# Rotary embedding's swapped halves: products on TensorE, or SBUF-to-SBUF copies with signed sine tables

## The reference, cut to what matters

```
x1, x2 = jnp.split(xa, 2, axis=-1)
return jnp.concatenate([x1 * cos - x2 * sin, x1 * sin + x2 * cos], axis=-1)
```

## Time and profile before

| | |
|---|---|
| median of 3 executions | 3674.78 us (3674.26 to 3675.93) |
| the profiled execution | 3672.84 us |
| its span | 3671.0 us |
| TensorE busy | 3589.8 us, 98% |
| VectorE, ScalarE, GpSimd busy | 51%, 41%, 10% |
| granted TensorE clock, mean | 0.993 |
| DMA | 337 MB, 92 GB/s in the mean |

### The profile page before, as it was taken

The page is one execution under the profiler, slowest core; times in us unless marked ns, Lnnn a source line. Parts: engine busy times, 40 slices in busy tenths (PEclk is TensorE's granted clock), DMA queues, the critical chain, the costliest instruction groups (busy, mean ns, idle before and its releaser), DMA issues.

```text
span 3671.0 us, 45622 instructions
## 1 busy us (share of the span) xinstructions
PE 3589.8 (98%) x18488; PEld 3002.9 (82%) x18488; DVE 1888.5 (51%) x3061; ACT 1506.3 (41%) x2534; POOL 382.5 (10%) x305
## 2 busy tenths in 40 slices
PE   8999999999999999999999999999999999999999
PEld 6898889999979777888757678888886777888887
DVE  4738797666665465445554443433346444343333
ACT  4245544444452463233455342332335634234232
POOL 0000042222210000000100101110100000111011
PEclk8999999999999999999999999999999999999999
DMA  6510232222244232233211223333321122332222
GB/s 254 177 47 1 107 129 64 69 69 70 62 165 138 70 118 88 90 103 101 69 49 53 84 86 96 100 104 92 98 89 52 47 85 72 100 104 94 98 93 86
DMA packets 112530, 337.12 MB, mean 92 GB/s; under 512 B 11840, under 2 KB 29120, under 8 KB 111808
## 3 DMA queue, kind: packets, MB, share of 16 engines
q1 hardware_dynamic: 103824, 301.70, 25.8%
q10 hardware_dynamic: 8496, 32.51, 2.5%
HBM read 330.49 MB, written 2.10 MB: 91 GB/s over the span
## 4 chain that ended last, share of the span: by engine, by line
PE 84%; DVE 6%; ACT 2%; issue 1%; ACTq 0%; DVEq 0%
PE ps L803 53%; PE ps L1167 8%; PE ps L1219 5%; PE ps L856 4%; PE ps L839 2%; PE ps L1532 1%; PE ps L1331 1%; PE ps L1322 1%; PE ps L1343 1%; PE ps L1073 1%; PE ps L1535 1%; PE ps L1576 1%; PE ps L1590 1%; PE ps L1005 1%; PE ps L1549 1%
## 5 line engine op out<-in xcount | busy, mean ns | idle before, releaser
L2694 DVE TENSOR_TENSOR wlo<-raw,whi 128x1024 fp32r<-128x1024 f32 (+3 forms) x583 | 620.7, 1067 | 638.1 <-ACT whi L1701 632.9
L1701 ACT ACTIVATE whi<-raw 128x1024 fp32r<-128x1024 f32 (+3 forms) x583 | 524.4, 902 | 723.5 <-PE ps L803 433.9
L803 PE MATMUL ps<-bh,whi 128*128 128x512 f32 x1248 | 496.4, 398 | 0.1
L803 PE MATMUL ps<-bh,wlo 128*128 128x512 f32 x1248 | 486.7, 390 | 0.5 <-DVE wlo L2694 0.5
L803 PE MATMUL ps<-bl,whi 128*128 128x512 f32 x1248 | 486.3, 390 | 0.0
L803 PEld LDWEIGHTS ps<-bh,whi 128*128 128x128 f32 x1248 | 234.7, 188 | 58.7 <-issue 8.1
L803 PEld LDWEIGHTS ps<-bl,whi 128*128 128x128 f32 x1248 | 234.8, 188 | 51.0 <-issue 3.4
L803 PEld LDWEIGHTS ps<-bh,wlo 128*128 128x128 f32 x1248 | 234.5, 188 | 50.3 <-DVE wlo L2694 1.0
L803 PE MATMUL ps<-ah,whi 128*128 128x384 f32 (+1 forms) x768 | 252.4, 369 | 8.0 <-DVE mod L2754 5.2
L803 PE MATMUL ps<-ah,wlo 128*128 128x384 f32 (+1 forms) x768 | 248.2, 363 | 0.1
L803 PE MATMUL ps<-al,whi 128*128 128x384 f32 (+1 forms) x768 | 248.0, 363 | 0.0
(11 more groups left out here) (480 smaller groups left out, 7391.1 us busy)
## 6 DMA issues: line engine op xcount, KB each, us to landing
raw<-weights_d SPq DMA_DIRECT2D x431, 512.0 KB, 3.5
aw<-ada_d ACTq DMA_DIRECT2D x56, 512.0 KB, 3.7
aw<-ada_d SPq DMA_DIRECT2D x40, 512.0 KB, 8.2
raw<-weights_d SPq DMA_DIRECT2D x80, 256.0 KB, 2.6
raw<-weights_d SPq DMA_DIRECT2D x44, 192.0 KB, 2.3
x<-nab_d SPq DMA_DIRECT2D x24, 256.0 KB, 2.8
x<-x_t_d SPq DMA_DIRECT2D x4, 1024.0 KB, 5.8
dt<-rtab_d SPq DMA_DIRECT2D x16, 256.0 KB, 2.9
```

The source lines that it names most:

```text
L803: m = e.matmul(p[:, 0:n], tiles(w, i)[:, k, :], xs[:, x0 + k, c0:c0 + n], start=pi == 0 and k == 0 and ti == 0, stop=i == job and k == kt ...
L1701: e.activation(flat(WHI, key), src, ACT.Copy).then_inc(q.did("hi", key))
L2694: e.tensor_tensor(flat(WLO, key), src, flat(WHI, key).bitcast(F32), ALU.subtract).then_inc(q.did("lo", key))
```

## The change

The products with PG and PR are taken out. In their place ScalarE, having evacuated a tile, issues four DMAs that copy 32 partitions of 512 fp32 values (64 KB) each to the place of the other half, in linear attention from the tile into gtr, in retention from RAW2 into RTM. The minus sign moves into the sine tables: in the constant SIN, and in the frequencies from which the kernel computes SINR. VectorE multiplies gtr or RTM by the sine in place; GpSimd's multiply by the cosine, which overwrites the source of the copies, waits for their landing. For tile 0 of retention ScalarE issues the copies after the end of stick-breaking attention. VectorE's and GpSimd's instructions are as many as before and in the same order.

```
-        cos[d], sin[d] = np.cos(ang), np.sin(ang)
+        cos[d], sin[d] = np.cos(ang), np.sin(ang) * (-1 if d % 64 < 32 else 1)
-    iv[:, 1] = np.tile(ir, 4)
+    iv[:, 1] = np.tile(ir, 4) * np.where(np.arange(128) % 64 < 32, -1, 1)
+    turned_in = [nc.alloc_semaphore(f"turned_in{i}") for i in range(4)]
+    swapped_in = [nc.alloc_semaphore(f"swapped_in{i}") for i in range(2)]
 # pe_program, linear attention
-        def rope(ct):
-            p = bank(4 + ct % 2, ("rtmp", ct))
-            q.wait_ge(("qk", ct), ("cg",))
-            e.matmul(p, PG, (Qt if ct < 4 else Kt)[:, ct % 4, TC:], start=True, stop=True, skip_group_check=True
-                     ).then_inc(q.did("ropemm", ct))
         lin_pair(["gla_w_in", "gla_w_in"], H, hr, HALF)
-        rope(0)
         for ct in range(2, 8):
             lin("gla_w_in", H, hr, HALF)
-            rope(ct - 1)
         lin("gla_a_w1", H, hr, HALF)
-        rope(7)
 # pe_program, retention
-            rotate(6, ("rq", l, 0), PR, RAW2[0], ("rraw", l, 0, 0))
-            rotate(7, ("rk", l, 0), PR, RAW2[1], ("rraw", l, 0, 1))
...
                 lin("w_in_2", B, br, ONE)
-                rotate(0, ("rq", l, j + 1), PR, RAW2[0], ("rraw", l, j + 1, 0))
                 ret_values(j, 2)
-                rotate(1, ("rk", l, j + 1), PR, RAW2[1], ("rraw", l, j + 1, 1))
                 lin("w_in_2", B, br, ONE)
 # act_program
+        def swap_halves(dst, src, sem, *name):
+
+            for to in range(0, 128, 32):
+                fro = to ^ 32
+                e.dma_start(dst[to:to + 32, :], src[fro:fro + 32, :]).then_inc(q.lands(sem, *name), 16)
+
         def evac_qk(i, ct):
...
             q.note("qk", ct)
+            q.wait_ge(("qk", ct), *([("rope", ct - 4)] if ct >= 4 else []))
+            swap_halves(GTR[ct % 4], (Qt if ct < 4 else Kt)[:, ct % 4, TC:], turned_in[ct % 4], "turned", ct)
...
+            def ret_swap(j, n):
+
+                q.wait_ge(("rraw", l, j, n), *([] if j else f))
+                swap_halves(RTM[n], RAW2[n], swapped_in[n], "swapped", l, j, n)
+
             def ret_raw(j, n):
...
                 q.note("rraw", l, j, n)
+                if j:
+                    ret_swap(j, n)
...
             q.note(f"end_sb{l}", "act")
             f = fence(f"end_sb{l}")
+            for n in range(2):
+                ret_swap(0, n)
 # dve_program
         def rope(ct):
             x = (Qt if ct < 4 else Kt)[:, ct % 4, TC:]
-            q.wait_ge(("ropemm", ct), ("cg",), *(f0 if ct < 4 else [("rope", ct - 4)]))
-            e.tensor_tensor(GTR[ct % 4], PS[4 + ct % 2], SIN, ALU.mult).then_inc(q.did("rtmp", ct))
+            q.wait_ge(("turned", ct), ("cg",))
+            e.tensor_tensor(GTR[ct % 4], GTR[ct % 4], SIN, ALU.mult).then_inc(q.did("rtmp", ct))
             q.wait_ge(("rcos", ct), ("rtmp", ct))
...
-                name, dst, b = (("rq", RQ), ("rk", RK))[n] + (n if j else 6 + n,)
+                name, dst = (("rq", RQ), ("rk", RK))[n]
                 free = f if j < 2 else [("rs", l, j - 2, 2)]
-                rotate(b, (name, l, j), RAW2[n], COSR, SINR, RTM[n], *(f if j == 0 else [(name, l, j - 1)]))
+                q.wait_ge(("swapped", l, j, n), ("cos", 1))
+                e.tensor_tensor(RTM[n], RTM[n], SINR, ALU.mult).then_inc(q.did("rot0", name, l, j))
 # pool_program
-            q.wait_ge(("ropemm", ct), ("cg",))
+            q.wait_ge(("turned", ct), ("cg",))
...
-                rotate(("rq", l, j), RAW2[0], COSR)
-                rotate(("rk", l, j), RAW2[1], COSR)
+                for n, name in enumerate(("rq", "rk")):
+                    q.wait_ge(("swapped", l, j, n), ("cos", 1))
+                    e.tensor_tensor(RAW2[n], RAW2[n], COSR, ALU.mult).then_inc(q.did("rotc", name, l, j))
```

## The result

| | before | after |
|---|---|---|
| median | 3673.7 us (3673.11 to 3675.93, 6 runs) | 3699.22 us (3694.19 to 3700.69, 6 runs) |
| profiled execution, its span | 3672.84, 3671.0 us | 3699.86, 3698.1 us |
| granted clock, mean | 0.993 | 0.987 |

The ratio is 1.0068, with a 95% interval of 1.0057 to 1.0078: slower by some 25 us, where 9 us of gain were forecast, and outside the range. The spans differ by 27.1 us.

The account below looks back on a forecast made before the run. TensorE was taken to bound the kernel, busy 3589.8 of 3671.0 us. Products -21.0, first rotation +8.7, clock +2.3 and retention's rotations +1.0 gave -9.0 us: median 3665.8 us, range 3652 to 3674.

Parts of the forecast that it names:

- The products, -21.0: Linear attention and retention: removing 24 permutation products from TensorE's path saves 21.0 us (6.9, 3.8 and 10.3).
- Rival D: Whole kernel: the removed products stood beside something else that takes as long; chance 0.14 shared with B.
- The first rotation, +8.7: Linear attention: swap lands at 75.5, delays VectorE's low half of chunk 3; TensorE stalls 8.7 us (5.5 to 10.7).
- The collision of VectorE with GpSimd: First rotation, linear attention: multiplies and add run one after another, up to 4.0 us instead of 2.0.
- Rival A: Linear attention: no stall at the first rotation, copies land at 68 despite the loads; 3655.3 us, chance 0.25.
- The clock there, +2.3: Linear attention, behind the first rotation's stall: TensorE's granted clock falls to 0.50, costing 2.3 us.
- Retention's tile rotations, +1.0: Retention, tiles 1 to 3: scores wait for the rotated key 0.2 us at each of six tiles, about 1 us.
- L: Retention: landing time of the key's swap copies, taken as 2.7 us, ends 2.0 and 5.1.
- B: Retention: key swap becomes a new wait at six tiles, L 3 to 4, up to 9 us; chance 0.14 with D.
- C: Retention: copies land so late that the kernel slows; L over 5.4 to lose 7.3 us; chance 0.06.
- ScalarE's issues, 0: ScalarE's queue: 96 copy issues at 0.48 us, 46 us in all, cost nothing on the path.

Follow-up runs that it names:

- e9: Kernel before, products kept on TensorE, with three retention reorderings (low half earlier, last decay product earlier, values' third bank evacuated first): 3673.47 us, ratio 1.0002.
- e8: e5 plus VectorE's last decay product ahead of the previous tile's normalization and ScalarE evacuating the values' third bank first: 3652.40 us, ratio 0.9950.
- e6: e1 with the conditioning vector and the first five loads of its product issued by SyncE instead of ScalarE: 3671.23 us, ratio 0.9995.
- e1: Kernel before with the change in linear attention alone, retention's products kept on TensorE: 3679.29 us, ratio 1.0020.
- e4: Changed kernel with retention's low half of tile j - 1 on VectorE ahead of the key's rotation instead of behind it: 3674.34 us, ratio 1.0009.
- e5: e4 with VectorE's first rotation in linear attention also moved behind the low halves of chunks 3 and 4: 3666.22 us, ratio 0.9980.

## Why the prediction was wrong, by its own steps

- **The products, -21.0.** Right. With this price the table closes within some 3 us for all kernels but two, and the pair with the smallest changes beside it gives nearly the same: from e9 to e8 the span falls by 18.4 us with 1.6 us more waits and 0.8 more clock sum, which leaves 20.0 to 20.8 us for the products. The one place where it was too high by itself: tile 0's two products had covered ScalarE's evacuation of the values (rv), and without them TensorE waits 1.8 us there, in each layer; of the 3.8 us only some 0.3 came in. Rival D, right for 3.5 us.
- **The first rotation, +8.7.** The mechanism was right, the size too small: 11.4 us, over the upper bound of 10.7. The landing came at 78.4, not 75.5 (bound 77.5): that is the term that was mis-sized. The collision of VectorE with GpSimd is there: 1.74 us for the add, 0.69 elsewhere, while GpSimd was at its multiplies (three in 4.66 us from 78.52). Rival A is out; e6 shows that a copy queued behind large loads lands some 5 us earlier when they are on the other queue (72.8, against 78.0 in e1). Three of the changed kernel's four copies landed before the last load ahead of them on their queue did (75.4 to 76.1, against 77.7).
- **The clock there, +2.3.** The term was the author's estimate of 4.7 us at a granted clock of 0.50, the time from 44.23 to 49 of before; no run shows this term behind a stall. In its place the runs showed, of the same kind and a little smaller: from the end of the stall at 84.3 to 85 the grant was 0.50 and from 85 to 90 0.75, which loses 0.35 + 1.25 = 1.6 us; in e1, from 83.8 to 87 it was 0.50 and from 87 to 88 0.54, 2.1 us. It was counted at this place only.
- **Retention's tile rotations, +1.0.** The step that failed. It asked who needs the rotated key, found the scores with 7.4 us of cover, and priced L - 2.5. It didn't ask what is queued behind the waiting instruction. Behind it stood ret_low, with 1.6 us of slack to the mean, and there the price is L itself, at four places. With my own L of 2.7 that is 10.8 us, not 1.0; with the measured 3.1 to 4.8 it is 15.6. For the scores themselves L - 2.5 was about right: in e4, where the key's copies of tiles 2 and 3 landed in 4.1 and 3.4 us in layer 0, it gives 2.5 us a layer, and TensorE waited 5.7 in the two. The clock then fell at each of the waits on the mean; that term, at most 13.6 us in retention's windows, was missing altogether.
- **L, 2.7.** Too low where it mattered. A quiet queue lands 64 KB in 2.0 us, but at tiles 2 and 3 SyncE's loads of the decay tables and of a weight chunk stood on the engines: 4.7 and 3.4. Rivals B and C, given 0.14 and 0.06, had this place but the wrong consumer: B stopped at 9 us, and C asked for L over 5.4 before it would decide.
- **ScalarE's issues, 0.** About right on the path: the four issues take 2.45 us, and the last begins 1.84 us after the first, 0.5 more than at the 0.45 cadence; one issue took 0.61 us, not the 0.48 of rows 6.

By how much the clock costs in a single run stays open: the same kernel e5 ran between 3660 and 3672 us, with falls of the clock that come and go in stages that no edit touches (below). No run separates what sets them off.

## What to carry to other kernels

When an instruction gets a new wait, list what is queued behind it on its engine and follow each of these to TensorE, not only the reader of its own result. A buffer with one copy (ry) joins two tiles in such a chain. An offload that takes work from the bounding engine pays only where the landing has cover; here two changes of order on VectorE turned +25 us into -8, and a third into -17.

## What the runs showed of the hardware

- An SBUF-to-SBUF copy of 64 KB over 32 partitions took 0.61 us of ScalarE's queue to issue (median of 32 and of 64), against 0.48 for a 512 KB load, and landed 1.9 to 2.1 us after its issue on quiet queues, 10.8 to 12.5 us behind 3.6 MB on its own queue. Tile views of gtr and of rtm after:

```profile
L1862 ACTq DMA_DIRECT2D gtr<-gqk x32: 514/612/762, 63.8 to 129.7; - x32
...
DMA to landing us min/median/max: 1.9/2.1/12.5
```
```profile
DMA to landing us min/median/max: 1.9/2.0/4.7
```

- The clock also fell where nothing had changed. In the latent attention ahead of retention, the same waits of up to 1.7 us stood in both kernels. Before, the window there was at 1.00; after, at 0.91; in e9, whose linear and latent attention are those of before, the 20 us windows from 1880 to 1920 were at 0.91 again. Windows of before and of after:

```profile
1910.00:1930.00 20.00, 18.76 (x111) 14.33 (x110) 9.80 (x24) 12.93 (x26) 0.00 (x0) 1.00 0.18 54
```
```profile
1910.00:1930.00 20.00, 20.00 (x119) 15.66 (x118) 3.55 (x5) 7.84 (x14) 0.00 (x0) 0.91 0.19 53
```

- Differences under about 5 us between two kernels of this kind can't be read from one profile, since the clock sum alone moves by more than that: 17.0 to 27.1 us in the four fastest kernels.
